# Moving 27 small constant loads from the queue of the weights to ScalarE's queue

## The chip, the cores and the metric

The kernel runs on one core of one Trainium2 chip, as one launch. The metric is the device time of a launch in microseconds (us); lower is better. The core has five engines that each run their own instruction stream: TensorE (PE), VectorE (DVE), ScalarE (ACT), GpSimd (POOL) and SyncE (SP). They wait for one another through semaphores. Transfers run on 16 DMA engines that all queues share; in this kernel SP and ACT issue them.

## The reference

Two stacks of layers are applied one after the other to 256 tokens of width 1024, all in float32. The first has an attention and gating mixer, a pooling mixer, cross attention and a mixture of 16 experts per layer. The second is a conditioned two-layer transformer: each of its layers starts from a modulation vector, a product of a condition vector with a large matrix. Only that product and the tables around it matter here:

```python
cond_lat = jax.nn.silu(c)
cond_ctx = jax.nn.silu(c_ctx)
for i in range(DEPTH):                                # DEPTH = 2
    mod = (cond_lat @ ada_w[i] + ada_b[i])[:, None, :]     # ada_w[i] is 1024 x 6144
    modc = (cond_ctx @ ada_w[i] + ada_b[i])[None, None, :]
    sh1, sc1, g1, sh2, sc2, g2 = jnp.split(mod, 6, axis=-1)
    csh1, csc1, cg1, csh2, csc2, cg2 = jnp.split(modc, 6, axis=-1)
    h = modulate(rmsnorm(x, norm1_g[i]), sh1, sc1)
    hc = modulate(rmsnorm(xc, norm1_g[i]), csh1, csc1)
    ...                                               # attention, gated feed-forward
```

`ctx_2` is the second input stream (256 x 1024) on which the kernel's first layer works. `silu(c)` and `silu(c_ctx)` have to exist before the first product with `ada_w` can run.

## The kernel before, in words

The program is written by hand, one instruction stream per engine, with a counter semaphore for each hand-over. Nothing reorders it: within an engine, instructions start in the order in which they are written, and an instruction that waits holds all that stand behind it.

**The start.** `loads` is a list of 34 small transfers. The first seven (`N_COLIN`) are the two condition vectors, an identity matrix and four sets of norm weights (tile `colin`). ACT issues them at L1386, and PE waits for them (`colin_landed`) before its first instruction. The other 27 (`N_SETUP`) are 13 rows spread over 128 partitions (tile `bc`), the router's weights (`rw`), the positions (`pos_i`), and twelve pieces of `ada_b` (into `KT`). They count up `setup_landed`, for which ACT and DVE wait.

**The condition chain.** PE transposes the condition vectors (L735). ACT applies silu (L1390, tile `cond`; a load of the function's table stands ahead of it, and only the ACTIVATE waits for PE). PE spreads the result (L739), and DVE writes `spread_c` (L1946), which is the stationary operand of every product with `ada_w`.

**The modulation.** `ada_w` is read as 64 tiles of 768 KB (two layers of 32, `MOD_TILES`) into four slots of the buffer `raw` (`RAW` = 4). SP issues them at L485. From the fifth on it waits until PE has used the tile that stood in the slot four before (`ada_used`). PE does three products per tile (L754; the profile counts each in two records). Then DVE adds the biases (L1974, `mod_sum`), ACT writes the sums out (L1397) and reads them back (L1403), and the main layers begin: SP issues the weight tiles (L365), ACT makes their high part (L1162, tile `w_hi`), POOL their low part (L537, `w_lo`), and PE multiplies (L586 to L588).

SP's stream at the start is: four tiles of `ada_w`, the 27 small loads, `ctx_2` into `X` (L490), then the other 60 tiles of `ada_w`.

Of the kernel before, what the change touches and what calls it, by code (L numbers as in the profile page):

```python
# [57 lines left out]
N_COLIN = 7  # L58
# [91 lines left out]
def build(nc, A, out):  # L150
    ctx = ExitStack()
    with ctx:
# [72 lines left out]
        colin_landed, setup_landed, x_landed, tab_landed, prm_landed = \  # L225
# [115 lines left out]
        for layer in range(2):  # L341
            for _, n, rows in mod_parts:
                loads.append((mod_sums[layer][rows, :], bias[layer, n]))
# [6 lines left out]
        def _(sp):  # L350
# [126 lines left out]
            def modulation(layer, first, last):  # L477


                rows = ada[layer].rearrange("(i r) (g w) -> i (r g) w", r=32, g=4)  # L480
                for i in range(first, last):
                    a = layer * MOD_TILES + i
                    if a >= RAW:
                        sp.wait_ge(ada_used, a - RAW + 1)
                    sp.dma_start(raw[:, a % RAW, 0:MOD_COLS], rows[i]).then_inc(ada_landed[a % RAW], 16)  # L485

            modulation(0, 0, RAW)
            for dst, src in loads[N_COLIN:]:
                sp.dma_start(dst, src, allow_slow_non_contiguous=True).then_inc(setup_landed, 16)
            sp.dma_start(X[:, :, :], A["ctx_2"][0].rearrange("(t p) d -> p t d", p=P)).then_inc(x_landed, 16)  # L490
            modulation(0, RAW, MOD_TILES)
            modulation(1, 0, MOD_TILES)
# [65 lines left out]
        def _(pe):  # L558
# [127 lines left out]
            def attention(n, s_groups, scores, n_chunks, pv):  # L686
# [15 lines left out]
                def prob(i, _):  # L702
                    return PB[:, i % 4, :] if s_groups == 1 else PB[:, 2 * (i % 2), :]
# [107 lines left out]
            def cross(layer):  # L811
                to_at(H)
                gemm_t(4)
                gemm(2)
                to_at(X)
                gemm_t(4)

                def scores(i, _, bank):
                    h, t = divmod(i, 2)
                    for j in range(2):  # L820
                        ins = pe.matmul(bank[:, 0:TOK], QT[:, 2 * h + j, t * P:(t + 1) * P], KT[:, 2 * h + j, 0:TOK],
                                        start=j == 0, stop=j == 1)
                    return ins

                def pv(i):
                    h, t = divmod(i, 2)
                    if t == 0:
                        return
                    bank = o_bank()
                    for dc in range(2):  # L830
                        for kc in range(2):
                            at = h * 256 + dc * P
                            ins = pe.matmul(bank[:, dc * TOK:(dc + 1) * TOK], V[:, kc, at:at + P], PT[:, h % 2, kc, :],
                                            start=kc == 0, stop=kc == 1)
                    ins.then_inc(o_full, 1)
                attention(8, 1, scores, lambda i: 2, pv)
                pe.wait_ge(y_freed, c.get("y"))
                gemm(2)
# [310 lines left out]
        def _(act):  # L1149
# [234 lines left out]

            for dst, src in loads[:N_COLIN]:
                act.dma_start(dst, src, allow_slow_non_contiguous=True).then_inc(colin_landed, 16)  # L1386
            c.add("full", 2)
            act.wait_ge(wb_full, 2)
            bank()
# [1043 lines left out]
```

## Time and profile before

| what | value |
|---|---|
| median of 3 runs | 2493.68 us (2493.03 to 2502.45) |
| the profiled execution, its own time | 2493.63 us |
| its span from first to last instruction | 2491.8 us |
| busy share: PE, POOL, ACT, DVE | 79%, 36%, 28%, 34% |
| DMA, mean over the span | 193 GB/s |

The span is 1.8 us shorter than the execution's own time. All start times below are counted from the start of the span. A busy share is a mean over the whole span and says nothing of one stage; what a stage is bound by has to be read from that stage's rows.

### The profile page before, as it was taken

Reading aid. Unit: us, or ns where it says so; the run is one execution under the profiler, and the core shown is the slowest. Engines: PE = TensorE matmul, PEld = TensorE weight load, DVE = VectorE, ACT = ScalarE, POOL = GpSimd, SP = SyncE. Lnnn points to the kernel's source line nnn. Section 1 sums busy time; section 2 is a strip of 40 time slices with the busy share of each in tenths; the row PEclk is TensorE's granted clock in tenths of the full one; section 3 lists DMA queues with packets and bytes.
Section 4 is the critical chain, followed back from the end, with each engine's and each line's share of the span. In section 5 each row is a group of like instructions: output and inputs, shape, how many; then the busy total and the mean of one; then the engine's idle time right before and its main releaser. Section 6 shows DMA issues by size and latency. Waiting matters only on the chain.

```text
span 2491.8 us, 27534 instructions
## 1 busy us (share of the span) xinstructions
PE 1969.5 (79%) x10882; PEld 1472.7 (59%) x10882; DVE 851.2 (34%) x1502; ACT 703.2 (28%) x984; POOL 908.7 (36%) x199
## 2 busy tenths in 40 slices
PE   4667679977688779996698699958576999666998
PEld 0046479966378544444587444426445998535997
DVE  0038631133731311114232311137984111773111
ACT  1033344442323200002223100022253444333442
POOL 0056058855047000004462000034402778413884
PEclk9998889988589889997899799988797999788999
DMA  8975046644135359995444299993402566312562
GB/s 320 411 287 187 15 127 186 185 152 148 34 118 178 109 219 409 409 409 207 141 163 152 90 409 409 409 336 108 123 1 76 153 185 202 106 34 76 173 182 84
DMA packets 286433, 481.31 MB, mean 193 GB/s; under 512 B 17184, under 2 KB 176144, under 8 KB 285936
## 3 DMA queue, kind: packets, MB, share of 16 engines
q1 hardware_dynamic: 276560, 458.87, 52.1%
q10 hardware_dynamic: 9760, 20.88, 2.5%
q8 instruction: 79, 1.29, 0.2%
q14 instruction: 34, 0.28, 0.0%
HBM read 475.92 MB, written 3.77 MB: 193 GB/s over the span
## 4 chain that ended last, share of the span: by engine, by line
PE 46%; DVE 17%; DMA 6%; ACT 3%; issue 2%; SPq 1%; DVEq 0%; ACTq 0%
PE PS L586 10%; PE PS L587 10%; PE PS L588 10%; PE PS L919 7%; DMA raw<-l_e_up 3%; PE PS L894 3%; DMA V<-l_e_up 3%; DVE PB L1820 2%; DVE at_lo L1614 2%; DVE H L1808 2%; PE PS L962 1%; DVE st L1885 1%; ACT at_hi L1210 1%; DVE X L1748 1%; DVE X L1699 1%
## 5 line engine op out<-in xcount | busy, mean ns | idle before, releaser
L537 POOL TENSOR_TENSOR w_lo<-raw,w_hi 128x2048 fp32r<-128x2048 f32 x195 | 908.5, 4671 | 1557.8 <-ACT w_hi L1162 1557.7
L1162 ACT ACTIVATE w_hi<-raw 128x2048 fp32r<-128x2048 f32 x195 | 370.7, 1909 | 395.1 <-PE PS L588 372.9
L586 PE MATMUL PS<-at_hi,w_hi 128*128 128x256 f32 x1328 | 383.3, 289 | 32.9 <-DVE at_lo L1614 32.9
L587 PE MATMUL PS<-at_lo,w_hi 128*128 128x256 f32 x1328 | 382.0, 288 | 0.0
L588 PE MATMUL PS<-at_hi,w_lo 128*128 128x256 f32 x1328 | 381.7, 287 | 0.0
L586 PE MATMUL PS<-w_hi,at_hi 128*128 128x512 f32 (+1 forms) x640 | 260.7, 407 | 79.8 <-DVE at_lo L1614 41.2
L586 PEld LDWEIGHTS PS<-at_hi,w_hi 128*128 128x128 f32 x1328 | 261.5, 197 | 36.5 <-DVE at_lo L1614 35.5
L587 PEld LDWEIGHTS PS<-at_lo,w_hi 128*128 128x128 f32 x1328 | 261.6, 197 | 1.1
L588 PEld LDWEIGHTS PS<-at_hi,w_lo 128*128 128x128 f32 x1328 | 261.3, 197 | 0.0
L587 PE MATMUL PS<-w_lo,at_hi 128*128 128x512 f32 (+1 forms) x640 | 257.6, 403 | 0.0
L588 PE MATMUL PS<-w_hi,at_lo 128*128 128x512 f32 (+1 forms) x640 | 256.8, 401 | 0.0
L586 PEld LDWEIGHTS PS<-w_hi,at_hi 128*128 128x128 f32 x640 | 127.2, 199 | 113.2 <-DVE at_lo L1614 44.4
L1842 DVE TENSOR_TENSOR PB<-PB,PS 128x256 f32<-128x256 f32 x66 | 27.8, 421 | 431.1 <-ACT PB L1249 431.1
L919 PE MATMUL PS<-raw,KT 128*64 128x512 f32 x576 | 129.3, 595 | 18.8 <-DMA raw<-l_e_up 16.5
L588 PEld LDWEIGHTS PS<-w_hi,at_lo 128*128 128x128 f32 x640 | 126.3, 197 | 27.0
L587 PEld LDWEIGHTS PS<-w_lo,at_hi 128*128 128x128 f32 x640 | 126.8, 198 | 26.0
L754 PE MATMUL PS<-raw,spread_c 128*8 128x512 f32 x384 | 74.0, 662 | 54.6 <-DMA raw<-ada_w 53.8
L606 PE MATMUL PS<-ident,H 128*128 128x128 f32 x176 | 35.3, 380 | 96.2 <-DVE H L1766 75.3
L586 PE MATMUL PS<-w_hi,he_hi 128*128 128x512 f32 x264 | 103.1, 390 | 0.0
L587 PE MATMUL PS<-w_lo,he_hi 128*128 128x512 f32 x264 | 103.1, 390 | 0.0
L588 PE MATMUL PS<-w_hi,he_lo 128*128 128x512 f32 x264 | 102.7, 389 | 0.0
L919 PEld LDWEIGHTS PS<-raw,KT 128*64 128x64 f32 x576 | 46.8, 137 | 94.4 <-issue 92.9
(260 smaller groups left out, 2410.5 us busy)
## 6 DMA issues: line engine op xcount, KB each, us to landing
raw<-ffn_w_gu SPq DMA_DIRECT2D x132, 512.0 KB, 4.9
raw<-ada_w SPq DMA_DIRECT2D x64, 768.0 KB, 6.4
raw<-l_e_gate SPq DMA_DIRECT2D x80, 512.0 KB, 10.9
raw<-ffn_w_down SPq DMA_DIRECT2D x66, 512.0 KB, 4.1
raw<-l_e_up SPq DMA_DIRECT2D x64, 512.0 KB, 8.3
raw<-diff_w_in SPq DMA_DIRECT2D x48, 512.0 KB, 5.1
raw<-l_e_down SPq DMA_DIRECT2D x48, 512.0 KB, 13.7
H<-l_e_down SPq DMA_DIRECT2D x40, 512.0 KB, 12.7
```

The costliest lines, as they stand in the source:

```text
L537: nc.gpsimd.tensor_tensor(w_lo[:, n % RING, :], raw[:, n % RAW, :], w_hi[:, n % RING, :].bitcast(F32), ALU.subtract).then_inc(lo_done, 1)
L586: pe.matmul(dst, s_hi, m_hi, start=first, stop=False)
L587: pe.matmul(dst, s_hi, m_lo, start=False, stop=False)
L588: return pe.matmul(dst, s_lo, m_hi, start=False, stop=last)
L606: ins = pe.transpose(bank[:, j * P:(j + 1) * P], src[:, t, k * P:(k + 1) * P], ident[:, :])
L754: ins = pe.matmul(PS[32 * n:32 * n + 8, layer, :], spread_c[:, i, :], raw[:, a % RAW, n * 512:(n + 1) * 512], start=i == 0, stop=i == MOD_ ...
L894: ins = pe.matmul(PS[:, 6 + k // 4, (k % 4) * P:(k % 4 + 1) * P], Xk[:, t, k // 2, k % 2, :], onehot_t[:, t, :], start=t == 0, stop=t == N ...
L919: ins = pe.matmul(PS[r, bank, :], xe[p % 2][:, 4 * h + k, r], tiles[e][:, k * 512:(k + 1) * 512], start=h == 0 and k == 0, stop=h == 1 and ...
L1162: nc.scalar.activation(w_hi[:, n % RING, :], raw[:, n % RAW, :], ACT.Copy).then_inc(hi_done, 1)
L1614: return dve.tensor_tensor(dst, src, hi.bitcast(F32), ALU.subtract)
L1808: (ready if signal else D1)(dve.tensor_tensor(v[:, t, :, :], v[:, t, :, :], g, ALU.mult))
L1820: D1(dve.tensor_tensor(r4[:, :, :, b, :], v4[:, :, :, 1 - b, :], s4[:, :, b, :].unsqueeze(1).to_broadcast([P, n, 2, q]), ALU.mult))
```

## The change

The loop over `loads[N_COLIN:]` goes out of SP's stream and into ACT's, behind the loop over the first seven. Nothing is added or dropped: the same 34 loads, the same semaphores, the same waits. Only the issuing engine of 27 loads changes, and with it the place that they take in the order of each of the two engines.

```diff
@@ block.sync, start of the stream
             modulation(0, 0, RAW)
-            for dst, src in loads[N_COLIN:]:
-                sp.dma_start(dst, src, allow_slow_non_contiguous=True).then_inc(setup_landed, 16)
             sp.dma_start(X[:, :, :], A["ctx_2"][0].rearrange("(t p) d -> p t d", p=P)).then_inc(x_landed, 16)
             modulation(0, RAW, MOD_TILES)
             modulation(1, 0, MOD_TILES)
@@ block.scalar, start of the stream
             for dst, src in loads[:N_COLIN]:
                 act.dma_start(dst, src, allow_slow_non_contiguous=True).then_inc(colin_landed, 16)
+            for dst, src in loads[N_COLIN:]:
+                act.dma_start(dst, src, allow_slow_non_contiguous=True).then_inc(setup_landed, 16)
             c.add("full", 2)
             act.wait_ge(wb_full, 2)
             bank()
             nc.scalar.activation(cond[:, :], bank()[0:32, 0:64], ACT.Silu).then_inc(act_step, 1)
```

On ACT, at the start of the program, these rows stood in a row before (the first two are the last of the seven loads, the third and fourth the table load and the silu):

```order
L1386 DMA colin<-l_pool_scale 8x128
L1386 DMA colin<-l_sgu_b 8x128
L1390 ACT_TABLE_LOAD
L1390 ACTIVATE cond<-PS 32x64
L1210 ACTIVATE rw_hi<-rw 128x128
```

In the changed kernel these rows stand at the same place of ACT's stream, the last of the 27 loads and what follows them (line numbers below the removed lines are smaller by two):

```order
L1386 DMA bc<-c_invf 128x8
L1386 DMA bc<-c_before 128x16
L1386 DMA rw<-router_w 128x8x16
L1386 DMA pos_i<-positions 128x2x1
L1386 DMA KT<-ada_b 4x512 x12
L1390 ACT_TABLE_LOAD
L1390 ACTIVATE cond<-PS 32x64
L1208 ACTIVATE rw_hi<-rw 128x128
```

The table load and the silu, which stood directly behind the seven loads, now stand behind all 34.

On SP, the end of the small loads and what follows them stood like this before:

```order
L489 DMA rw<-router_w 128x8x16
L489 DMA pos_i<-positions 128x2x1
L489 DMA KT<-ada_b 4x512 x12
L490 DMA X<-ctx 128x2x1024
L485 DMA raw<-ada_w 128x1536 x60
L365 DMA raw<-diff_w_in 128x2x512 x24
```

In the changed kernel SP's stream begins with these rows:

```order
L349 UNCONDITIONAL_BRANCH
L485 DMA raw<-ada_w 128x1536 x4
L488 DMA X<-ctx 128x2x1024
L485 DMA raw<-ada_w 128x1536 x60
L365 DMA raw<-diff_w_in 128x2x512 x24
```

The load of `X` and the fifth tile of `ada_w` now stand directly behind the first four tiles.

## Rows read from the trace of the kernel before

**Rows 1.** Page: 40 slices of the span, TensorE clock and DMA
```profile
PEclk9998889988589889997899799988797999788999
DMA  8975046644135359995444299993402566312562
```

**Rows 2.** Waits, 0 to 150 us (total us, times, longest)
```profile
PEld PS L754 <- DMA raw<-ada_w: 113.9, 59, 9.5
```

**Rows 3.** Timeline of SP's queue, 0 to 62 us (start, us)
```profile
0.75 2.20 SPq L485 DMA_DIRECT2D raw<-ada_w  x4
2.99 0.49 SPq L489 DMA_DIRECT2D bc<-l_sinks  x1
...
7.21 1.00 SPq L489 DMA_DIRECT2D bc<-diff_lambda_k  x1
...
11.06 5.44 SPq L489 DMA_DIRECT2D pos_i<-positions  x1
16.54 4.58 SPq L489 DMA_DIRECT2D KT<-ada_b  x12
21.16 0.40 SPq L490 DMA_DIRECT2D X<-ctx  x1
```

**Rows 4.** DMA engines, 10.4 to 22.4 us
```profile
GB/s 185 107 40 31 15 21 48 38 44 36 36 15 105 134 77 41 46 65 64 53 23 30 22 74 54 37 21 30 85 113 118 78 34 27 27 27 27 21 7 205
DMA packets 3272, 0.68 MB, mean 57 GB/s; under 512 B 2818, under 2 KB 3203, under 8 KB 3272
```

**Rows 5.** Timeline of all engines, the start: ACT's queue and its first work
```profile
1.67 0.45 ACTq L1386 DMA_DIRECT2D ident<-c_ident  x1
2.14 1.60 ACTq L1386 DMA_DIRECT2D colin<-norm_g  x2
4.38 0.28 ACTq L1386 DMA_DIRECT2D colin<-l_sgu_b  x1
4.69 1.28 ACT L1390 ACT_TABLE_LOAD   x1 [4.69 <-issue]
11.22 0.34 PE L733 MATMUL PS<-ident,colin 48*128 48x48 f32 x1 [11.22 <-DMA colin<-l_sgu_b]
11.70 0.21 ACT L1390 ACTIVATE cond<-PS 32x64 f32<-32x64 f32 x1 [5.72 <-PE PS L735]
13.67 5.69 PE L754 MATMUL PS<-raw,spread_c 128*8 128x512 f32 x24 [0.61 <-DVE spread_c L1946]
14.48 0.15 PEld L754 LDWEIGHTS PS<-raw,spread_c 128*8 128x8 f32 x3 [0.70 <-issue]
```

**Rows 6.** Timeline of all engines: the later tiles and the end of the stage
```profile
22.45 0.31 ACT L1210 ACTIVATE rw_hi<-rw 128x128 fp32r<-128x128 f32 x1 [10.53 <-DMA KT<-ada_b]
27.89 0.12 PEld L754 LDWEIGHTS PS<-raw,spread_c 128*8 128x8 f32 x6 [9.47 <-DMA raw<-ada_w]
...
59.41 1.04 PE L754 MATMUL PS<-raw,spread_c 128*8 128x512 f32 x6 [0.81 <-DMA raw<-ada_w]
60.49 76.01 SPq L485 DMA_DIRECT2D raw<-ada_w  x40
...
81.88 2.10 DVE L1974 TENSOR_TENSOR KT<-KT,PS 8x512 f32<-8x512 f32 x3 [47.95 <-PE PS L754]
...
142.62 1.04 PE L754 MATMUL PS<-raw,spread_c 128*8 128x512 f32 x6 [0.90 <-DMA raw<-ada_w]
143.79 2.10 DVE L1974 TENSOR_TENSOR KT<-KT,PS 8x512 f32<-8x512 f32 x3 [15.22 <-PE PS L754]
145.93 1.98 ACTq L1397 DMA_DIRECT2D mods_d<-KT  x6
```

**Rows 7.** Busy time of PE by stretch, with clock, DMA share, GB/s
```profile
27.80:90.00 62.20, 37.88 (x192) 0.92 1.01 408
90.00:143.80 53.80, 32.45 (x185) 0.97 1.01 409
```

**Rows 8.** Transfers of the tensor ada_w, issue to landing
```profile
DMA to landing us min/median/max: 4.3/6.4/10.2
```

## The prediction

> **What bounds the kernel now.** I first read the page's 40 slices of about 62 us each [rows 1]. The DMA digit of the first slices is 8 and 9 while TensorE has nothing but the products with `ada_w`, so the start is a stage of its own. The list of waits for 0 to 150 us says who is late there: 59 waits of PE for tiles of `ada_w`, 113.9 us in all [rows 2]. The busy time by stretch confirms it: from 27.8 to 143.8 us the 16 DMA engines are fully busy at 408 to 409 GB/s, with PE at some 60% [rows 7]. The tiles from the fifth on come one after the other: the fifth is used at 27.89, the last at 142.62 [rows 6], so 59 intervals take 114.73 us, or 1.94 us a tile. Its bytes say the same: 0.786 MB at 409 GB/s are 1.92 us. Behind the last tile a strict chain follows (DVE's sum at 143.79, ACT's write-out at 145.93 [rows 6], then the first weight products). So whatever moves the fifth tile's landing moves the kernel's end by the same amount, unless the stream stalls later; nothing in the stage can catch up, since its limit is the transfer rate.
>
> Before the fifth tile there is a hole. From 10.4 to 22.4 us the DMA engines move only 57 GB/s in 3272 mostly tiny packets [rows 4]. SP is busy issuing the 27 small loads from 2.99 to 21.16 us, 18.17 us in all; the load of `X` goes out at 21.16 and the fifth tile behind it [rows 3]. That is the hole that the change is about. The question is what opens the stream in the changed kernel.
>
> **What is removed from SP.** All 18.17 us. SP then issues `X` at about 3.0 us, behind the first four tiles. `X` is 1.05 MB, so at 409 GB/s it takes 2.6 us on the DMA engines. That time used to stand directly ahead of the fifth tile, and is now spent before PE has used anything: it leaves the path. But SP cannot issue the fifth tile early. It waits until PE has used the first one. Before, that wait was long over when SP came to it (PE began at 13.67 [rows 5], SP arrived past 21). Now it decides.
>
> **What is added to ACT.** The 27 issues stand ahead of the silu that feeds `spread_c`, which every product needs. An ACT issue holds ACT as an SP issue holds SP: the last of the seven loads begins at 4.38 and takes 0.28, and the table load begins at 4.69 [rows 5]. For the durations of the 27 there are SP's rows: 0.49 for an ordinary one, 1.00 for one of them, 5.44 for the positions, 4.58 for twelve pieces of `ada_b` [rows 3]. ACT's own prices are the same in kind: 0.45 for the identity, 0.80 each for the two loads of norm weights [rows 5]. I take SP's total. ACT then ends issuing at 4.69 + 18.17 = 22.86.
>
> **The sum.**
> - The table load was covered: it ran from 4.69 for 1.28 us, while ACT waited for PE until 11.70 [rows 5]. That cover is gone, since PE's transposes will be ready (they started at 11.22; `X` on the other queue adds at most its 2.6 us to that, to 13.8). So the silu starts at 22.86 + 1.28 + 0.1 = 24.2, against 11.70.
> - From silu to the first product is 13.67 - 11.70 = 1.97 us [rows 5]. First product at 26.2.
> - PE releases the first slot when its products end. The next tile's weight load started 0.81 us after the first product (14.48 [rows 5]); with the tail of the last product I take 1.0. SP issues the fifth tile at 27.2.
> - It lands after the shortest time that a tile shows from issue to landing, 4.3 us [rows 8], as the DMA engines are empty then. Lands at 31.5. Before it was used at 27.89 [rows 6], behind `X`.
> - Difference +3.6 us. From there both run at 1.94 us a tile. PE frees the next slots 0.85 us apart, faster than tiles land, so four are in flight again at once.
>
> Own time of the profiled execution 2493.63 + 3.6 = 2497.2; the median of the runs is 0.05 above that execution, so 2497.3.
>
> **What is costed at nothing.** The 27 loads' own landing moves from 22.45 (ACT's first use [rows 6]) to about 24.2 or later. DVE's sum, the last user with a deadline, comes at 81.88 after 47.95 us of idle time [rows 6], which hides a lateness of 24 us and more. PE starting later than 13.67 uses only the four tiles that have landed anyway.
>
> **Bounds of the unknown price.** The uncertain term is how long ACT takes to issue. Low: the positions cost 5.44 because the queue was full (SP's queue held four tiles and 14 small loads; the packets of the small ones were still draining until 22 us [rows 4]), and ACT's queue, which holds no large tiles, takes them for an ordinary 0.49. ACT ends 4.95 us earlier, and the difference is 3.6 - 4.95 = -1.4 us: 2492.3. High: the small packets drain later, as `X` is now ahead of them on the shared engines (2.6 us more), and ACT is held until then: +6.2 us, 2499.9. I take the middle, SP's own total, because ACT's queue gets the same 27 loads in the same order and the slow drain [rows 4] is of those very packets.
>
> **A rule beside it.** The trace shows 18.17 us of SP's time in these issues [rows 3] and the tiles waiting behind them. The Trainium skill, page DMA: Bandwidth & Descriptors, section Issuing engines are not separate DMA queues, says that starting transfers from several engines only saves the time in which the sequencer starts them, and that this is usually small beside the transfer itself. By that sentence the change could only save; it does not speak of what the second sequencer has standing behind the issues, and here that sequencer feeds PE. If it holds as it stands, it is the first rival below.
>
> **Rivals.**
> 1. *ACT's issues do not delay the silu* (it waits for PE until 11.70 anyway, and would overlap them). Then PE starts at 13.67, SP issues the fifth tile at 14.7, it lands at 19.0, and the gain is 8.9 us: 2484.8. For it: the hole is real and 8.9 us wide. Against it: 4.38 + 0.28 followed by 4.69 [rows 5] shows ACT in order. Chance 0.05.
> 2. *The positions' 5.44 us were SP's full queue and vanish on ACT.* 2492.3 as above. For it: all ordinary loads cost 0.5. Against: they went out before the drain of small packets had begun in earnest. Chance 0.17.
> 3. *Slower by more than can be mistaken: ACT issues each small load at the price of its contended ones.* Two queues compete until the first four tiles and `X` have passed, and ACT's two loads of norm weights took 1.60 [rows 5], 0.80 each. At 0.80 for 26 loads and 5.44 for the positions ACT is busy for 26.2 us, 8.1 more than in the sum: 2505.4. It decides (over 0.5%) from a mean of about 0.83. Against it: the identity took 0.45 and the last of the seven 0.28 in the same stretch. Chance 0.08, of which half beyond 0.5%.
> 4. *The forecast*, ACT held 17 to 21 us: +2 to +6.5. Chance 0.70.
>
> **How the numbers follow.** A measurement of this kernel tells a change from none at about 0.5%, 12.5 us, that is outside 2481.2 to 2506.2. The forecast and rivals 1 and 2 lie inside; so does half of rival 3. The runs before spread over 9.4 us upward, and PE's granted clock, which moves between 0.5 and 0.9 by slices [rows 1], may fall otherwise when all is shifted; a few in a hundred on either side for that. Faster 0.02, same 0.92, slower 0.06. The range goes from just below rival 2 to below rival 3, with some of that spread: 2489 to 2503.
>
> **What would show it.** In the changed profile: SP issues `X` near 3 us and then waits for PE (a wait of SP for L754 of over 20 us); ACT's queue is busy from 0.75 to about 23; the table load starts there and not at 4.69; silu at about 24; PE's first product with `ada_w` at about 26, the fifth tile near 31.5; and all of the later stages 3 to 4 us later, the last tile at about 146. The DMA engines stand nearly idle between 13 and 28 us. The prediction is wrong if the silu starts before 18 us (rivals 1, 2) or after 28 (rival 3), or if the positions' issue takes under 1 us, or if the tiles behind the fifth do not keep 1.94 us.

## The result and the profile after

The changed kernel is slower: median 2504.03 us (8 runs, 2498.55 to 2506.56) against 2494.68 us (8 runs, 2492.54 to 2502.45) for the kernel before in the same comparison. The ratio is 1.0031, with a 95% interval of 1.0018 to 1.0045, or 4.5 to 11.2 us with 7.7 in the middle. The sign and the mechanism were those of the forecast; its 3.6 us lie below that interval.

The timeline of all engines of the changed kernel, 0 to 36 us (start, duration), answers to [rows 3] and [rows 5]:

```profile
2.90 0.44 SPq L488 DMA_DIRECT2D X<-ctx  x1
...
4.49 0.36 ACTq L1386 DMA_DIRECT2D bc<-l_sinks  x1
...
9.58 2.02 ACTq L1386 DMA_DIRECT2D bc<-diff_lambda_k  x1
11.23 0.34 PE L731 MATMUL PS<-ident,colin 48*128 48x48 f32 x1 [11.23 <-DMA colin<-l_sgu_b]
...
13.14 5.67 ACTq L1386 DMA_DIRECT2D pos_i<-positions  x1
18.84 5.59 ACTq L1386 DMA_DIRECT2D KT<-ada_b  x12
24.46 1.28 ACT L1390 ACT_TABLE_LOAD   x1 [24.46 <-issue]
25.76 0.21 ACT L1390 ACTIVATE cond<-PS 32x64 f32<-32x64 f32 x1
...
27.72 7.21 PE L752 MATMUL PS<-raw,spread_c 128*8 128x512 f32 x30 [0.61 <-DVE spread_c L1946]
...
29.66 5.66 SPq L485 DMA_DIRECT2D raw<-ada_w  x5
...
33.87 0.14 PEld L752 LDWEIGHTS PS<-raw,spread_c 128*8 128x8 f32 x6 [0.91 <-DMA raw<-ada_w]
```

PE had finished its transposes by 12 us, and ACT had their input. But ACT was issuing loads until 24.46; only then came the table load and the silu. PE stood idle for almost 15 us, and so did SP, as the list of SP's waits, 0 to 150 us, shows (total us, times, longest):

```profile
SPq L485 <- PE PS L752: 119.7, 60, 26.3
```

The longest wait, 26.3 us, is the one for the first slot. What the DMA engines did in the end of it, 24.5 to 31 us (40 slices):

```profile
GB/s 0 50 0 50 0 0 0 0 0 0 0 0 0 0 0 0 0 0 0 0 0 0 0 0 0 0 0 0 0 0 0 0 0 0 0 0 0 38 492 76
```

All small packets had landed, and the engines were idle until the fifth tile's first packets. That is what the change has added: before, the hole had the small loads in it [rows 4] and closed at about 22 us; now it has the same small loads, and over 5 us of nothing behind them. It also closes more slowly than before. The stretches from 30 to 40 us (busy time of PE, clock, DMA share, GB/s), first of the changed kernel, then of the kernel before:

```profile
30.00:34.00 4.00, 4.00 (x21) 1.00 0.85 246
34.00:40.00 6.00, 2.22 (x18) 1.00 0.93 329
```

```profile
30.00:34.00 4.00, 3.17 (x18) 0.81 1.02 416
34.00:40.00 6.00, 3.42 (x24) 1.00 1.02 420
```

Before, all four slots were free when SP came to them, and it issued four tiles in a row. Now each of the first tiles behind the hole waits for PE to free a slot, 1.7 us apart. So the changed kernel is 6.0 us late at the fifth tile and 8.1 at the eighth (41.64 against 33.54). From there on it loses nothing more.

The end of the stage (timeline, 138 to 170 us) answers to [rows 6], the stretches with clock, DMA share and GB/s to [rows 7]:

```profile
149.85 1.04 PE L752 MATMUL PS<-raw,spread_c 128*8 128x512 f32 x6 [0.88 <-DMA raw<-ada_w]
151.01 2.10 DVE L1974 TENSOR_TENSOR KT<-KT,PS 8x512 f32<-8x512 f32 x3 [14.82 <-PE PS L752]
```

```profile
90.00:150.00 60.00, 35.88 (x206) 0.97 1.01 410
```

The last tile is used at 149.85, 7.2 us later than before. That agrees with the 7.7 us of the ratio (4.5 to 11.2). The profiled execution itself (span 2496.6) is the fastest of the eight and shows a span only 4.8 us longer, as it spent 2.4 us less behind the last tile than the profiled execution of before; the other seven took 2502.09 to 2506.56.

### The profile page after: what moved, and what is told of

The parts are those of the page before. It is cut to its first block, busy times and chain, and to the rows that moved or that the text cites. A ratio compares the mean times of both kernels' runs of the same rounds, so it can differ in the third digit from the quotient of the medians.

```text
span 2496.6 us, 27534 instructions
## 1 busy us (share of the span) xinstructions
PE 1967.4 (79%) x10882; PEld 1472.0 (59%) x10882; DVE 852.3 (34%) x1502; ACT 703.0 (28%) x984; POOL 909.7 (36%) x199
## 4 chain that ended last, share of the span: by engine, by line
PE 46%; DVE 17%; DMA 6%; ACT 3%; issue 2%; SPq 1%; DVEq 0%; ACTq 0%
PE PS L584 10%; PE PS L585 10%; PE PS L586 10%; PE PS L917 7%; DMA raw<-l_e_up 3%; DMA V<-l_e_up 3%; PE PS L892 3%; DVE PB L1820 2%; DVE at_lo L1614 2%; DVE H L1808 2%; PE PS L960 1%; DVE st L1885 1%; ACT at_hi L1208 1%; DVE X L1748 1%; DVE X L1699 1%
## 5 line engine op out<-in xcount | busy, mean ns | idle before, releaser
L1842 DVE TENSOR_TENSOR PB<-PB,PS 128x256 f32<-128x256 f32 x66 | 27.8, 421 | 431.5 <-ACT PB L1247 431.5
## 6 DMA issues: line engine op xcount, KB each, us to landing
H<-l_e_down SPq DMA_DIRECT2D x40, 512.0 KB, 12.7
```

## The experiments

Eleven kernels were run, each compared with the kernel before on the same chip. This table has each one's silu, the time at which SP issued the fifth tile, the fifth tile's first use, the last tile's (all from the timelines of the profiled executions), and the ratio of the times.

| kernel | silu | 5th issued | 5th used | last used | ratio (95%) |
|---|---|---|---|---|---|
| before | 11.70 | 21.6 | 27.89 | 142.6 | 1 |
| changed | 25.76 | 29.66 | 33.87 | 149.8 | 1.0031 (1.0018 to 1.0045) |
| e1 silu first | 11.71 | 15.61 | 23.47 | 146.9 | 1.0003 (0.9991 to 1.0015) |
| e2 X first, loads on SP | 10.38 | 23.85 | 28.03 | 145.3 | 1.0003 (0.9994 to 1.0013) |
| e3 positions on SP | 22.96 | 26.86 | 31.08 | 152.5 | 1.0029 (1.0009 to 1.0048) |
| e4 half ahead of the silu | 13.67 | 17.58 | 27.71 | 142.6 | 0.9996 (0.9986 to 1.0007) |
| e5 loads on POOL | 15.91 | 19.82 | 24.09 | 143.2 | 1.0000 (0.9989 to 1.0011) |
| e6 conditions on SP, silu first | 4.94 | 8.85 | 18.90 | 142.4 | 0.9980 (0.9968 to 0.9992) |
| e7 e1 without the 13 rows of bc | 11.61 | 15.52 | 20.17 | 137.9 | 0.9963 (0.9949 to 0.9977) |
| e8 e6 with seven loads late | 4.25 | 8.59 | 21.22 | 139.8 | 0.9980 (0.9970 to 0.9989) |
| e9 e6 with bc spread by PE | 5.09 | 9.01 | 16.99 | 136.3 | 0.9953 (0.9938 to 0.9968) |
| e10 changed, bc spread by PE | 15.99 | 19.89 | 24.34 | 148.1 | 0.9985 (0.9974 to 0.9995) |
| e12 before, bc spread by PE | 10.76 | 14.67 | 20.30 | 135.7 | 0.9975 (0.9964 to 0.9986) |

The column "last used" is of one execution each and does not follow the ratio closely: e10 used its last tile 5.5 us later than the kernel before, at a ratio of 0.9985, in an execution that was the slowest of its twelve. So for sizes the ratios count; the columns to its left tell the mechanism. In e6, e8 and e9 the fifth tile is issued while the first tiles and `X` are still being moved, and PE waits 3.2 to 5.1 us for it behind the fourth.

### Does the silu's place cost the time? (e1, e4)

e1 puts the same 27 loads behind the silu; e4 puts 13 ahead and 14 behind.

```diff
             for dst, src in loads[:N_COLIN]:
                 act.dma_start(dst, src, allow_slow_non_contiguous=True).then_inc(colin_landed, 16)
+            for dst, src in loads[N_COLIN:20]:          # only in e4
+                act.dma_start(dst, src, allow_slow_non_contiguous=True).then_inc(setup_landed, 16)
-            for dst, src in loads[N_COLIN:]:
-                act.dma_start(dst, src, allow_slow_non_contiguous=True).then_inc(setup_landed, 16)
             c.add("full", 2)
             act.wait_ge(wb_full, 2)
             bank()
             nc.scalar.activation(cond[:, :], bank()[0:32, 0:64], ACT.Silu).then_inc(act_step, 1)
+            for dst, src in loads[N_COLIN:]:            # loads[20:] in e4
+                act.dma_start(dst, src, allow_slow_non_contiguous=True).then_inc(setup_landed, 16)
```

> The 27 loads stay on ACT's queue, but behind the silu. Theory (the silu's place behind the loads holds the stream): silu back at 11.7 us, first product at 13.7, fifth tile of ada_w issued at about 15.6 and used at about 20, last tile some 8 us earlier than the 142.6 of the kernel before; the small packets now run beside the stream and may give back up to 6 us of that, so 2 to 8 us under the kernel before (ratio 0.997 to 0.999). Rival (the loss comes from the small packets on a second queue, or from X going first, whatever the place of the silu): not faster than the kernel before, ratio 1.000 to 1.003.

> On ACT the 13 spread rows of bc go ahead of the silu, the other 14 loads (router, positions, ada_b) behind it. Theory (each us of ACT's issuing ahead of the silu is a us of the stream): issues end at 12.7, silu at 14.0, first product at 15.9, fifth tile issued at 17.9 and used at 22.2; 11.8 us under the changed kernel, 2.3 us over the one with the silu ahead of all 27. Rival (the place of the silu has no price): like the changed kernel.

Measured: 1.0003 and 0.9996. Both are faster than the changed kernel, e4 by 1.0031 - 0.9996 = 0.35% or 8.7 us with intervals that don't touch. So the order on ACT is the cause of the loss: e1 has the same queues, the same packets and `X` in the same place, and differs in nothing else. But only the first half of the theory's expectation came in. e1 brought the fifth tile's issue forward to 15.61 as computed, and gained nothing against the kernel before, where 2 to 8 us were expected. The tile needed 7.9 us from issue to use (23.47), where 4.3 were reckoned. e4 should have used it at 22.2 and been 2.3 us slower than e1; it issued it at 17.58, used it at 27.71, 10.1 us later, and was not slower. A second cost had to be there. The timeline of e1, ACT's queue and SP's, 0 to 60 us:

```profile
11.71 0.21 ACT L1388 ACTIVATE cond<-PS 32x64 f32<-32x64 f32 x1 [5.95 <-PE PS L733]
11.71 0.36 ACTq L1390 DMA_DIRECT2D bc<-l_sinks  x1
...
15.61 44.25 SPq L485 DMA_DIRECT2D raw<-ada_w  x20
...
20.87 7.93 ACTq L1390 DMA_DIRECT2D pos_i<-positions  x1
28.83 4.23 ACTq L1390 DMA_DIRECT2D KT<-ada_b  x12
```

The loads are issued beside the stream until 33 us, and share its engines. But it is not only the engines' time that they take. The DMA engines of e4 from 17.6 to 22 us, with the packets, MB and share of each queue that had any (q10 is ACT's, q1 SP's):

```profile
DMA  9379656221301001220002211001201100014457
DMA packets 944, 0.16 MB, mean 37 GB/s; under 512 B 904, under 2 KB 944, under 8 KB 944
q10 hardware_dynamic: 944, 0.16, 28.9%
```

SP had issued the fifth tile at 17.58, and not one of its packets ran before 22 us, though the engines were busy for 29% of that time, all with ACT's small packets. e1 shows the same from 15.6 to 19.8 us: 522 packets of ACT's queue, none of SP's.

### What do the small packets cost? (e7, with e1)

e7 is e1 without the 13 loads into `bc`; it leaves their values out and has a constant in their place.

```diff
-            for dst, src in loads[N_COLIN:]:
+            for dst, src in loads[20:]:
                 act.dma_start(dst, src, allow_slow_non_contiguous=True).then_inc(setup_landed, 16)
@@ block.vector, start
             D1(dve.memset(ms[:, 4:5], RMS_EPS))
+            D1(dve.memset(bc[:, :], 0.0625))
```

> The kernel with the silu first, with the 13 loads into bc left out (bc is filled with a constant by DVE, so the norm weights and biases of it are not the right ones). Theory (the packets of the broadcast rows keep the DMA engines from the tiles): the fifth tile, issued at 15.6, is used at about 20 in place of 23.5, and the last one 3 to 7 us earlier than in that kernel. Rival (the router, the positions and ada_b are what costs, or the stream's own unevenness): within 2 us of it.

Measured 0.9963: 10 us under e1 by the ratios, and the last tile is used 9.0 us earlier, above the 3 to 7 expected. The other values of `bc` did not shorten what follows: behind the last tile's first product e7's span goes on for 2350.8 us, e1's for 2347.5. The fifth tile, issued at 15.52, is used at 20.17, after 4.65 us in place of 7.9. All of this difference lies ahead of its first packet, which runs about 1 us after the issue in e7 and 4.3 us after it in e1. The DMA engines from 15.6 to 40 us, first in e1, then in e7:

```profile
DMA packets 4030, 7.25 MB, mean 297 GB/s; under 512 B 2506, under 2 KB 2890, under 8 KB 4030
```

```profile
DMA packets 1686, 9.03 MB, mean 370 GB/s; under 512 B 200, under 2 KB 200, under 8 KB 1686
```

In e1 the engines carry 1.78 MB less, which is 4.4 us of the stream at its 409 GB/s [rows 7]. The later start of the fifth tile, 3.2 us, is the larger part of it. The rest is time on the engines: from 20 to 36 us ACT's queue has 2126 packets in e1, which take 12.7% of them for 0.28 MB. So the 13 rows, only 3.3 KB of data spread over 128 partitions as 1664 packets, cost the stream twice: a tile issued behind them on the other queue starts late, and then they share the engines with it. What holds the tile back while the engines have room was not tested. In the kernel before the rows ran in the hole, where they were partly free. That is where e1's expected gain went: it is 4.4 us ahead of the kernel before at the fifth tile, and 0.6 us at the twelfth (40.51 against 41.12). e7 is 5.8 us ahead of e1 at the twelfth; the other 3 of its 9.0 us arise later, when few small packets are left (137 from 36 to 45 us), and stay open.

### What are the 5.7 us of the positions? (e3, e7, e10)

```diff
+            sp.dma_start(loads[21][0], loads[21][1], allow_slow_non_contiguous=True).then_inc(setup_landed, 16)
@@ block.scalar
-            for dst, src in loads[N_COLIN:]:
+            for dst, src in loads[N_COLIN:21] + loads[22:]:
```

> The changed kernel with the positions' load alone moved back to SP, behind X. If its 5.67 us on ACT are the price of its own shape (256 elements of 4 bytes), ACT ends issuing at 18.8, silu at 20.1, first product at 22.0: 5.7 us under the changed kernel. If they are the price of a full queue, the load behind it inherits them: the first piece of ada_b takes some 5 us, silu at 25, and the time is that of the changed kernel within 1 us.

The measured times lie between the two expectations. The timeline of e3, SP's queue and ACT's:

```profile
3.40 0.53 SPq L489 DMA_DIRECT2D pos_i<-positions  x1
...
12.40 0.47 ACTq L1387 DMA_DIRECT2D rw<-router_w  x1
12.91 8.72 ACTq L1387 DMA_DIRECT2D KT<-ada_b  x12
```

On SP the load costs 0.53, so its shape is not the price. The twelve pieces of `ada_b` behind it on ACT now take 8.72 in place of 5.59 and inherit 3.1 of the 5.67 us; the silu comes 2.8 us earlier. The ratio, 1.0029, can't tell that from nothing. e7 and e10 settle it from the other side. With the `bc` rows left out the positions cost 0.60 on ACT (e7), and with them replaced 1.14 (e10). On SP without the `bc` rows ahead it costs 0.58 (e12), with them 5.44 [rows 3]. So the wait comes with the spread rows that stand ahead of it in its queue, in SP's before as in ACT's after; that it is a wait for room in that queue fits all of this, but no run shows a queue's room. The rows are not all of it: in e9, which has none, the twelve pieces of `ada_b` took 8.79 us beside the tiles, in e10 4.33, all ahead of the fifth tile's issue.

### Is X's move worth its 2.6 us? (e2)

```diff
             modulation(0, 0, RAW)
+            sp.dma_start(X[:, :, :], A["ctx_2"][0].rearrange("(t p) d -> p t d", p=P)).then_inc(x_landed, 16)
             for dst, src in loads[N_COLIN:]:
                 sp.dma_start(dst, src, allow_slow_non_contiguous=True).then_inc(setup_landed, 16)
-            sp.dma_start(X[:, :, :], A["ctx_2"][0].rearrange("(t p) d -> p t d", p=P)).then_inc(x_landed, 16)
```

> The kernel before with one edit: X is issued ahead of the 27 loads on SP. Theory of the sum (X leaves the path): SP issues the fifth tile at 21.6 as before, it is used at about 26 in place of 27.9, 2 us gained (ratio 0.999). Rival: the small packets wait behind X, SP is held in the positions' issue 2.6 us longer, and nothing is gained (ratio 1.000).

Measured 1.0003: the rival. SP's small loads take 20.5 us in place of 18.17, the fifth tile is issued 2.3 us later, and it is used at 28.03 against 27.89. The positions' load took no longer (5.60); the time went into three rows of `bc` (1.03 to 1.38 each) and the pieces of `ada_b`. So what the fifth tile gains in landing without `X` ahead of it (4.2 us for 6.3), the issues ahead of it take. In the changed kernel this shows in the same way: ACT's issues took 19.97 us where SP's had taken 18.17.

### A queue where nothing waits (e5), and the conditions earlier (e6, e8)

e5 issues the 27 from POOL, ahead of its first tile work (the router's load in two halves, so 28 issues), and `X` stands first on SP. e6 is e1 with the condition vectors and the identity issued by SP ahead of the tiles; e8 is e6 with seven loads moved behind the first output projection's weights.

```diff
@@ e5: block.gpsimd
+            for dst, src in loads[N_COLIN:]:
+                pool.dma_start(dst, src, allow_slow_non_contiguous=True).then_inc(setup_landed, 16)
             lo_until(TOTAL)
@@ e6: block.sync, and loads[3:N_COLIN] on ACT
+            for dst, src in loads[:3]:
+                sp.dma_start(dst, src, allow_slow_non_contiguous=True).then_inc(colin_landed, 16)
             modulation(0, 0, RAW)
@@ e8: block.sync, behind gemm(diff_out, 0, D)
+            for n in LATE:                              # (7, 8, 12, 13, 18, 19, 21)
+                sp.dma_start(*loads[n], allow_slow_non_contiguous=True).then_inc(late_landed, 16)
```

> The 27 loads go out from POOL's queue (the router's load in two halves), where nothing waits behind them before 150 us; X goes first on SP. Theory (two costs: what stands behind the issues, and the DMA engines' time for the small packets): the first cost is gone, silu at 11.7 and the fifth tile issued at 15.6 as in the kernel with the silu first; the second stays, so the time is that kernel's within 2 us (ratio 0.999 to 1.001). Rival (the issuing sequencer is the only cost): the fifth tile is used at 20, the last at 135, ratio 0.997.

> Silu ahead of the 27 loads, and the two condition vectors and the identity issued by SP ahead of the tiles, so that they don't compete with them; ACT issues the four sets of norm weights, then the silu, then the 27. Theory (the stream restarts 2 us after the first product plus a landing): the seven loads land by about 7 us in place of 11.2, first product at about 9.5, fifth tile issued at 11.5, when X is still on the DMA engines: no hole at all. The small packets still cost their time on the DMA engines; last tile 4 us under the kernel with the silu first, ratio 0.997 to 0.999 against the kernel before. Rival (the stage is bound by tiles and small packets together and the hole was paid by the small ones anyway): no gain over it.

> The kernel with the condition vectors on SP, and seven of the 27 loads (sinks, router bias, two gqa norms, the frequencies, the order table, the positions) issued by SP only behind the weights of the first output projection, where the DMA engines are almost idle; they are first used later. Theory (small packets cost the stream their time on the DMA engines): 2 to 4 us under the kernel it is derived from, ratio 0.995 to 0.998 against the kernel before. Rival (small packets are free there): same as it.

e5 came to 1.0000, as expected, but not by the expected path: its silu stood at 15.91. The first wait of its PE (timeline, 0 to 24 us) shows why:

```profile
15.43 0.34 PE L734 MATMUL PS<-ident,colin 48*128 48x48 f32 x1 [15.43 <-DMA colin<-l_sgu_b]
```

The seven loads of ACT landed 4.2 us later, with POOL's packets beside them from the start. e6 gained 5 us (0.9980), in the expected range: the silu is at 4.94, and of the hole there is left only a stretch from 10 to 12 us with the DMA engines busy for 0.72 of it. Its ACT queue, meanwhile, takes 9.48 us for the positions alone. e8 gained nothing over e6, where 2 to 4 us were expected. Seven of the thirteen spread rows and the router's load were still beside the stream; whether the moved ones gave back later what they saved was not tried.

### The spread rows done another way (e9, e10, e12)

The 13 rows go to one partition, and PE spreads them with a row of ones; the 27 loads stay where each parent kernel has them (e12: on SP; e10: on ACT ahead of the silu; e9: on ACT behind it, conditions on SP).

```diff
-                 (bc[:, B_SINK:B_SINK + 8], rowb(A["l0_sinks"])),
+                 (bc_row[:, B_SINK:B_SINK + 8], A["l0_sinks"].unsqueeze(0)),
...
@@ block.tensor
-            modulation(0, 0, MOD_TILES)
+            modulation(0, 0, 16)
+            pe.wait_ge(setup_landed, 16 * N_SETUP)
+            pe.matmul(PS[:, 2, :], ones_row, bc_row[:, 0:512], start=True, stop=True)
+            pe.matmul(PS[:, 3, 0:B_COLS - 512], ones_row, bc_row[:, 512:B_COLS], start=True, stop=True).then_inc(bc_full, 1)
+            modulation(0, 16, MOD_TILES)
@@ block.vector, behind rms_to_h()
+            dve.wait_ge(bc_full, 1)
+            D1(dve.tensor_copy(bc[:, 0:512], PS[:, 2, :]))
+            D1(dve.tensor_copy(bc[:, 512:B_COLS], PS[:, 3, 0:B_COLS - 512]))
```

> The kernel with the condition vectors on SP and the silu ahead of the 27 loads, with the 13 loads of bc going to one partition (one row each, 3.2 KB in all) and spread over 128 partitions by two PE products with a row of ones, behind tile 16, and two DVE copies. Theory (the 1664 packets of the spread rows fill the queue and keep the engines from the tiles): no load's issue takes over 2 us, the stream has no hole, last tile at 130 to 134 in place of 142.6, ratio 0.995 to 0.997. Rival (the stage stays bound by something else, or PE's wait costs what is gained): ratio 0.998, as without this edit.

> The changed kernel (silu behind all 27 loads) with the same edit of bc. Theory (the positions' 5.7 us on ACT are the wait for room in the queue that the spread rows fill, and each us of ACT's issuing is a us of the stream): the positions take under 1 us, ACT ends issuing at 15 to 17, first product at 18.5 to 20, fifth tile used at 25 to 26; 8 us under the changed kernel, ratio 0.998 to 1.000 against the kernel before. Rival (the issue times belong to the shapes): ACT ends past 21 and the ratio is over 1.001.

> The kernel before, all 27 loads on SP, with the same edit of bc alone. SP ends its small loads at 13 to 15, X behind them, the fifth tile then waits for PE's first product to end at 15.6 and is used at 20 to 22: 6 to 7 us under the kernel before, ratio 0.997 to 0.998. Against it the two kernels above show what the queue is worth once the small packets are few: the one with the silu behind the loads should be slower than this by 4 us, the early one faster by 3 to 5.

All three ratios fell in their ranges, though e9 used its last tile later than expected in the profiled execution (136.3 for 130 to 134). The timeline of e10, ACT's queue:

```profile
4.60 0.32 ACTq L1392 DMA_DIRECT2D PB<-l_sinks  x1
4.95 0.29 ACTq L1392 DMA_DIRECT2D PB<-router_bias  x1
...
9.17 1.14 ACTq L1392 DMA_DIRECT2D pos_i<-positions  x1
10.34 4.33 ACTq L1392 DMA_DIRECT2D KT<-ada_b  x12
...
15.99 0.21 ACT L1396 ACTIVATE cond<-PS 32x64 f32<-32x64 f32 x1
```

A one-partition row costs ACT 0.3 us in place of 0.5, no issue stalls for long, and all 27 are out at 14.7 in place of 24.46: with the silu still behind them, the kernel is 0.46% (11 us) under the changed one, where 8 us were expected. Against e12, which has the same loads on SP, it stays 0.10% behind (0.9985 and 0.9975, intervals overlapping; the order of the two is as expected, the size not proven). e9, with the silu early and the packets few, is the best of all: 0.9953, 12 us under the kernel before (0.9938 to 0.9968). The early order was worth 0.22% against e12, or 5.5 us, for 3 to 5 expected; the two intervals still touch at their ends (0.9968 and 0.9964).

## Why the prediction was right or wrong

**What binds the stage, and that the end moves with the fifth tile: right.** The fifth tile moved by 33.87 - 27.89 = 6.0 us, the last one by 7.2, the kernel by 7.7 (4.5 to 11.2).

**What is removed from SP, and the wait that takes its place: right.** `X` at 2.90, then a wait of 26.3 us for PE.

**What ACT is held up by: right in kind, short in size.** The sum had ACT issuing from 4.69 for 18.17 us, to 22.86. It was 4.49 to 24.46, or 19.97 us. The high bound's reason (the packets drain behind `X`, up to 2.6 us) was the right one for most of the 1.6 us of difference at the end; taking SP's own total as the middle ignored it. e2 shows the same 2 us on SP.

**The table load's lost cover: right,** 24.46 to 25.74, and 1.96 us from silu to the first product.

**The release of the first slot: the term that was too small.** The prediction took the weight load 0.81 us behind the first product [rows 5] as the end of the first tile's products, and so 1.0 us to the release. That weight load is the next tile's, but it does not wait for the first tile: the six weight loads of a tile are one group of "x6" at 13.67 in [rows 5], and the next group, of the second tile, begins at 14.48, while the second half of the tile's products is only starting. The first tile's six product records, PE alone, 28.5 to 29.3 us of the changed kernel:

```profile
27.72 1.89 PE L752 MATMUL PS<-raw,spread_c 128*8 128x512 f32 x6 [0.61 <-DVE spread_c L1946]
```

They end at 29.61, and SP issues at 29.66, 1.94 us after the first product. The same in e4: 15.64 to 17.58. The 1.89 us are the price of a tile at the lower level of the clock (last section); at the upper one it is 1.04, about what the prediction took.

**The landing: right.** 4.2 us for 4.3.

**The later pace: the second term, put at nothing.** The prediction had the next slots come free 0.85 us apart, so that four tiles would be in flight at once. That is half a tile; they came free 1.7 us apart, and the DMA engines were not full until about 40 us (246 and 329 GB/s above). From the fifth tile to the eighth the changed kernel took 7.73 us, the kernel before 5.64, so 2.1 us were lost there. From the eighth to the last it was 0.9 us faster than the kernel before. The mean over all 59 intervals, 1.97 us (33.87 to 149.84) for 1.94, hides both; it is 1.2 us in all.

Together: 1.6 for ACT's issues, 0.9 for the release and -0.1 for the landing are 2.4 us on the fifth tile, 1.2 behind it, and so 7.2 for 3.6. The mechanism held; the sum was half of what came.

**The numbers.** Slower within 0.5% was right: 0.31%. On the median from which the forecast was made, the ratio gives 2501.4 us, within 2489 to 2503. The median of the eight runs, 2504.03, is 1 us above the range, as those of the kernel before were 1 us higher too in that comparison.

**The rivals.** The first (silu not delayed) fell: ACT is strictly in order. But e1, which makes its premise true, shows that its 8.9 us were wrong as well: the hole was not empty, and the small packets take their time beside the tiles if not before them, and they delay the start of a tile that is issued behind them. That price was missing from the prediction altogether. The second (the positions' price vanishes on ACT) fell as a forecast, 5.67 us, while half of its reason was right: the price is that of what stands ahead in the queue. But it is the small rows and not the large tiles that make it, and ACT's queue had the same rows. The third did not occur: ordinary loads cost 0.36 to 0.54 on ACT, with one of 2.02.

**The rule beside it.** The Trainium skill, page DMA: Bandwidth & Descriptors, section Issuing engines are not separate DMA queues, says transfers of all issuing engines interleave on the same 16 DMA engines. On the engines the traces agree: in e1 from 20 to 36 us they move 2126 packets of ACT's queue and 934 of SP's. But the interleaving does not begin with the issue, as e4 shows, where SP's tile had no packet for 4.4 us. Its other half, that a second issuer only saves sequencer time, does not hold here as a bound on the effect: the second sequencer had the silu behind the issues, and the kernel lost 0.31%.

## What to carry to other kernels

An issue holds everything behind it on its engine, so before moving loads to an "idle" queue, look at the first compute instruction behind the place, who waits for it, and what that wait gates: here one 0.2 us silu gated PE, PE's release gated SP, and SP gated the stream. A hole in the DMA engines' use is not free room if small packets lie in it: closing it by moving the issues only moves the packets beside the large transfers, and can delay their start (4.3 us from issue to first packet in e1, 1 us in e7). Rows spread over 128 partitions by DMA are such packets; one row per load and a product with ones gave 0.25% on the kernel before, no less than the best order of the loads alone (e6, 0.20%), and the two add up (e9, 0.47%).

## What the runs showed of the hardware that was not expected

A load's issue has no fixed price. The positions' load of 1 KB took 0.53, 0.60, 1.14, 5.67, 7.93 and 9.48 us in e3, e7, e10, the changed kernel, e1 and e6: the short ones without spread rows ahead in the queue, the long ones behind them.

A transfer on one queue can be held up by small ones on the other without the engines being full: from 17.6 to 22 us of e4 the engines were busy for 29% and SP's issued tile had no packet. The cause stays open.

The stream of tiles is not evenly bound by transfers. In e10 the granted clock fell for a while in the middle of the stage. Busy time of PE by stretch, with clock, DMA share and GB/s:

```profile
36.00:48.00 12.00, 7.63 (x36) 0.86 1.00 407
48.00:54.00 6.00, 5.74 (x16) 0.52 1.01 399
54.00:60.00 6.00, 5.97 (x30) 0.63 0.74 253
60.00:66.00 6.00, 2.15 (x12) 0.94 0.92 331
```

At about 0.50 of full speed (the 1.2 GHz level) a tile takes PE 1.89 us, and 1.04 when the clock is up, by two rows of the timelines, of the kernel before (granted clock 0.50 from 27.8 to 30 us) and of e10:

```profile
27.90 1.89 PE L754 MATMUL PS<-raw,spread_c 128*8 128x512 f32 x6 [8.54 <-DMA raw<-ada_w]
```

```profile
45.82 1.04 PE L754 MATMUL PS<-raw,spread_c 128*8 128x512 f32 x6 [0.83 <-DMA raw<-ada_w]
```

A tile's transfer takes 1.92. So while the clock is low PE is no faster than the transfers. What else it has to do then (here the two products that spread `bc`, 3 us) frees slots late, and the DMA engines fall to 253 GB/s. The mean per tile was 1.94 us in the kernel before, 1.97 in the changed one and 2.09 in e1, in one execution each. Such stretches probably make up much of the few us by which runs of one kernel differ, but that was not tested.

The shown clock of the start should not be trusted. The first four tiles of the changed kernel took 1.7 us each (half tiles 0.82 to 0.86 us apart from 27.72 on), though their granted clock is shown as 1.00. The weight loads of the kernel before, whose first tiles are shown at 1.00 throughout as well, tell why:

```profile
17.05 0.15 PEld L754 LDWEIGHTS PS<-raw,spread_c 128*8 128x8 f32 x3 [0.70 <-issue]
17.90 0.10 PEld L754 LDWEIGHTS PS<-raw,spread_c 128*8 128x8 f32 x3 [0.70 <-issue]
18.33 0.10 PEld L754 LDWEIGHTS PS<-raw,spread_c 128*8 128x8 f32 x3 [0.33 <-issue]
```

Half tiles are 0.85 us apart up to 17.90 and 0.43 from there on, a factor of two. A tile whose granted clock is shown as 0.50 has the same 1.89 us as the first one (27.90 above). So PE ran its first products at the 1.2 GHz level, with only its few short transposes and the spreading product done before them, and rose to the upper one at about 17.9 us in the kernel before and at about 33 us in the changed kernel.
